# Decoders' attention in a hybrid decoder step: values moving past stationary weights in four column groups, and keys and small weights stored turned

## What is computed

```python
def _stick_breaking_block(q, k, v, q_pos, k_pos, sb_bias):
    z = jnp.einsum('bqhd,bkhd->bhqk', q, k).astype(jnp.float32) * (HEAD_DIM ** -0.5)
    z = z + sb_bias.astype(jnp.float32)[None, :, None, None]
    readable = k_pos[None, :] < q_pos[:, None]
    log_keep = jnp.where(readable, jax.nn.log_sigmoid(-z), 0.0)
    log_after = lax.cumsum(log_keep, axis=3, reverse=True) - log_keep
    weights = jnp.where(readable, jnp.exp(jax.nn.log_sigmoid(z) + log_after), 0.0)
    return jnp.einsum('bhqk,bkhd->bqhd', weights.astype(v.dtype), v)
```

## Time and profile before

| | |
|---|---|
| median of 3 runs | 2342.86 us (2342.21 to 2346.5) |
| profiled execution, whole time | 2343.74 us |
| its span, first to last instruction | 2342.0 us |
| mean granted TensorE clock | 0.88 |
| TensorE, VectorE, ScalarE, GpSimd busy | 79%, 66%, 24%, 55% |
| moved by the DMA | 844.78 MB, mean 361 GB/s |
| chain that ended last | PE 39%, DMA 24%, DVE 15%, POOL 6%, issue 6% |

### The profile page before, as it was taken

One profiled execution on the slowest core, in us unless ns is written; L12 is line 12 of the kernel. 1 busy time (PEld: TensorE's weight loads), 2 busy tenths in 40 slices (PEclk: granted clock), 3 DMA queues, 4 the chain that ended last, 5 costly groups with the idle time before them and its releaser, 6 DMA issues.

```text
span 2342.0 us, 24900 instructions
## 1 busy us (share of the span) xinstructions
PE 1858.9 (79%) x7896; PEld 1299.5 (55%) x7896; DVE 1555.9 (66%) x3451; ACT 557.2 (24%) x1184; POOL 1284.8 (55%) x1197
## 2 busy tenths in 40 slices
PE   4878889788897977979789999777665677677787
PEld 2658878667785755745667577665443222222233
DVE  1211265799878667788787565767789886776652
ACT  1041121566111221246122200110111221122121
POOL 0001044576656566667666435655566677767773
PEclk7999989889998988989987657999787899989999
DMA  8878799999999899999999798999998999999997
GB/s 290 315 278 258 268 334 354 408 357 328 382 411 412 332 402 344 412 411 351 395 410 409 288 312 299 408 394 330 388 404 324 335 386 408 391 409 408 409 409 264
DMA packets 218370, 844.78 MB, mean 361 GB/s; under 512 B 27135, under 2 KB 34615, under 8 KB 196736
## 3 DMA queue, kind: packets, MB, share of 16 engines
q0 software_dynamic: 167168, 605.66, 67.4%
q1 hardware_dynamic: 35044, 215.27, 23.9%
q10 hardware_dynamic: 16028, 22.26, 2.8%
HBM read 826.02 MB, written 16.80 MB: 360 GB/s over the span
## 4 chain that ended last, share of the span: by engine, by line
PE 39%; DMA 24%; DVE 15%; POOL 6%; issue 6%; DVEq 5%; ACT 3%; SPq 1%; ACTq 0%; POOLq 0%
PE bank L855 11%; DMA gather_ring<-in_expert_down,expert_numbers 10%; PE bank L846 9%; PE bank L1224 8%; DMA gather_ring<-in_expert_up,expert_numbers 5%; DVE expert_sums L1994 4%; DMA weight_chunks<-in_w_in 4%; DVE gather_ring L1963 4%; POOL gather_ring L811 3%; POOL gather_ring L796 2%; PE bank L1142 2%; PE bank L1139 1%; DMA v_tokens<-in_expert_up,expert_numbers 1%; DMA weight_chunks<-in_expert_down,expert_numbers 1%; DMA row_tables<-mod_prompt 1%
## 5 line engine op out<-in xcount | busy, mean ns | idle before, releaser
L796 POOL DMA_INDIRECT gather_ring<-in_expert_down,expert_numbers x510 | 588.9, 1155 | 518.3 <-DVE expert_dots L1963 259.8
L1224 PE MATMUL bank<-gather_ring,coef_diagonals 128*128 128x512 f32 x1040 | 575.6, 694 | 270.4 <-DMA gather_ring<-in_expert_up,expert_numbers 164.2
L811 POOL DMA_INDIRECT gather_ring<-in_expert_up,expert_numbers x532 | 570.4, 1072 | 312.1 <-PE bank L1224 145.3
L1963 DVE CUSTOM_DVE_ANT_0 gather_ring<-gather_ring,h_tiles 128x1024 f32<-128x1024 f32 x410 | 500.5, 1226 | 183.5 <-DMA gather_ring<-in_expert_down,expert_numbers 164.3
L1224 PEld LDWEIGHTS bank<-gather_ring,coef_diagonals 128*128 128x128 f32 x1040 | 212.0, 218 | 558.8 <-issue 418.9
L855 PE MATMUL bank<-hT,weight_chunks 128*128 128x128 f32 (+2 forms) x2304 | 401.5, 335 | 29.5 <-DMA weight_chunks<-in_w_in 21.1
L855 PEld LDWEIGHTS bank<-hT,weight_chunks 128*128 128x128 f32 x2304 | 371.7, 197 | 72.3 <-issue 36.5
L1994 DVE SCALAR_TENSOR_TENSOR expert_sums<-gather_ring,expert_coefs,expert_sums 128x1024 f32<-128x1024 f32 x269 | 345.5, 1284 | 8.6 <-issue 8.6
L846 PE MATMUL bank<-weight_chunks,hT 128*128 128x256 f32 x960 | 223.9, 393 | 25.2 <-DMA weight_chunks<-in_w_in 17.3
L846 PEld LDWEIGHTS bank<-weight_chunks,hT 128*128 128x128 f32 x960 | 188.2, 198 | 62.9 <-DMA weight_chunks<-in_w_in 20.3
L1541 ACT ACTIVATE coef_diagonals<-identity,expert_coefs 128x128 f32<-128x128 f32 x304 | 108.6, 395 | 357.6 <-DVE expert_coefs L1974 166.2
(11 more groups left out here) (268 smaller groups left out, 2154.3 us busy)
## 6 DMA issues: line engine op xcount, KB each, us to landing
weight_chunks<-in_w_in SPq DMA_DIRECT2D x84, 1024.0 KB
weight_chunks<-in_w_ada SPq DMA_DIRECT2D x24, 1024.0 KB
weight_chunks<-in_w_query SPq DMA_DIRECT2D x24, 1024.0 KB
weight_chunks<-in_w_branch_a SPq DMA_DIRECT2D x12, 1024.0 KB
weight_chunks<-in_w_branch_b SPq DMA_DIRECT2D x12, 1024.0 KB
weight_chunks<-in_w_out SPq DMA_DIRECT2D x12, 1024.0 KB
gather_ring<-in_expert_up,expert_numbers POOLq DMA_INDIRECT x532, 10.8
weight_chunks<-in_cache_k SPq DMA_DIRECT2D x16, 512.0 KB
```

The lines of the kernel that those rows point to most:

```text
L796: pool.indirect_dma_start(out=d_row(slot), out_offset=None, in_=down, in_offset=bass.IndirectOffsetOnAxis(ap=expert[:, t, h * TOPK + k:h * ...
L811: pool.indirect_dma_start(out=u_row(slot), out_offset=None, in_=up, in_offset=bass.IndirectOffsetOnAxis(ap=expert[:, t, h * TOPK + k:h * T ...
L1224: mm = nc.tensor.matmul(bank[6 + half], diag[:, n % 8, :], u_row(slot)[:, half * 512:(half + 1) * 512], start=(u == PE_TILE[t][0]), stop=( ...
L1963: nc.vector.tensor_tensor_reduce(out=row, in0=row, in1=x, scale=1.0, scalar=0.0, op0=ALU.mult, op1=ALU.add, accum_out=dots[:, m % 2, k:k + ...
```

## The change

1. The host stores `cache_k`, `w_spatial` and `sub_keys` turned, so that a page of keys arrives with the head's channels on the partitions. `turn_page`, the copies of `page_turned`, `turn_small` and the copies behind them are gone; `page_scores` reads the page in the weight buffer. The corner blocks are 8 loads instead of 16, straight into their place, and VectorE masks both in place.
2. The values' products change their operands: for each decoder, each half of the heads and each of three parts of keys, four products with 32 columns of weights stationary (those of four decoders, of which one is wanted) and 128 columns of values moving write four column groups of 32 partitions, one for each head. ScalarE sets the banks aside (`set_aside`), TensorE turns them, and 16 small copies pick the wanted blocks into `qT`. TensorE waits for them before the mix.
3. The exponents are three pieces instead of one, the costs in `pieces` are new, and two pieces "turn values" follow the values.

```diff
     if g == LASTG:
-        out += [("past scores", 9)] * NDEC + [("own scores", 6), ("exponents", 8)] + [("past values", 7)] * NDEC
+        out += [("past scores", 5)] * NDEC + [("own scores", 6)] + [("exponents", 7)] * 3
+        out += [("past values", 3)] * NDEC + [("turn values", 4)] * 2
...
-        ws_nat = U[:, 0:1024].rearrange("p (g s) -> p g s", g=NH)
-        wss_nat = U[:, 1024:2048].rearrange("p (g s) -> p g s", g=NH)
-        sk_nat = sg[:, 2, 0:256].rearrange("p (a d) -> p a d", a=2)
...
-        turned_page = [kT[:, j].rearrange("p h d -> p (h d)") for j in range(2)]
         kTf = kT[:, 2].rearrange("p h d -> p (h d)")
         pos_s = [kTf[:, 0:512], kTf[:, 512:1024], vv[0:NS, 2, 0:512]]
         neg_s = [vv[:, 0, 0:512], vv[:, 0, 512:1024], vv[0:NS, 2, 512:1024]]
-        log_s = [vv[:, 1, 0:512], vv[:, 1, 512:1024], turned_page[0][0:NS, 0:512]]
+        log_s = [vv[:, 1, 0:512], vv[:, 1, 512:1024], kT[0:NS, 0].rearrange("p h d -> p (h d)")[:, 0:512]]
+        side_s = [kT[:, 2 * n + 1].rearrange("p h d -> p (h d)") for n in range(2)]
...
                 elif phase == "keys":
-                    sp.wait_ge(s_ktf[1], 2 * c + 2)
+                    sp.wait_ge(s_sz, c + 1)
...
-            const(nc.gpsimd.memset(wss_nat, 0.0))
+            const(nc.gpsimd.memset(small_rows[0:NS, :], 0.0))
...
-            def turn_small(c):
-                if c == 0:
-                    pe.wait_ge(s_small, 16 * NSMALL)
-                    pe.wait_ge(s_wss, 16 * (P // DSEQ))
-                for half in range(2):
-                    if c < 2:
-                        turn_four(4 + 2 * c + half, [(ws_nat, wss_nat)[c][:, 4 * half + j, :] for j in range(4)])
-                    elif c == 2:
-                        turn_four(8 + half, [sk_nat[:, half, :]])
...
-                    def turn_page(m_):
-                        n = NUMBER["keys", g, m_ // 2]
+                    for b in range(NDEC):
+                        n = NUMBER["keys", g, b]
                         weight(n)
-                        page = row_of(n, m_ % 2)
-                        for half in range(2):
-                            if m_:
-                                pe.wait_ge(s_kte, 2 * (m_ - 1) + half + 1)
-                            for j in range(4):
-                                mm = nc.tensor.transpose(bank[2 + half][:, j * P:(j + 1) * P],
-                                                         page[:, (4 * half + j) * P:(4 * half + j + 1) * P], ident[:])
-                            mm.then_inc(s_ktf[half], 1)
-                    def page_scores(m_):
-                        b, page = m_ // 2, m_ % 2
-                        pe.wait_ge(s_kte, 2 * m_ + 2)
-                        for hd in range(NH):
-                            at = hd * NS + b * DSEQ
-                            mm = nc.tensor.matmul(bank[4 + page][:, at:at + DSEQ],
-                                                  turned_page[m_ % 2][:, hd * P:(hd + 1) * P],
-                                                  q[:, hd, P + b * DSEQ:P + (b + 1) * DSEQ], start=False,
-                                                  stop=(b == NDEC - 1 and hd == NH - 1))
+                        for page in range(2):
+                            for hd in range(NH):
+                                at = hd * NS + b * DSEQ
+                                mm = nc.tensor.matmul(bank[4 + page][:, at:at + DSEQ], row_of(n, page)[:, hd * P:(hd + 1) * P],
+                                                      q[:, hd, P + b * DSEQ:P + (b + 1) * DSEQ], start=False,
+                                                      stop=(b == NDEC - 1 and hd == NH - 1))
                         mm.then_inc(s_sz, 1)
-                    for b in range(NDEC):
-                        for m_ in (2 * b, 2 * b + 1):
-                            turn_page(m_)
-                            if m_:
-                                page_scores(m_ - 1)
                         yield
-                    page_scores(2 * NDEC - 1)
...
-                    mm.then_inc(s_scm, 1)
-                    yield
+                        mm.then_inc(s_scm, 1)
+                        yield
                     pe.wait_ge(s_sw, 1)
                     for b in range(NDEC):
                         n = NUMBER["values", g, b]
                         weight(n)
-                        for hd in range(NH):
-                            at = slice(hd * NS + b * DSEQ, hd * NS + (b + 1) * DSEQ)
-                            nc.tensor.matmul(bank[4][:, at], vv[0:NS, SAMPLE, hd * P:(hd + 1) * P], log_s[2][:, at],
-                                             start=True, stop=False)
-                            for page in range(2):
-                                mm = nc.tensor.matmul(bank[4][:, at], row_of(n, page)[:, hd * P:(hd + 1) * P],
-                                                      log_s[page][:, at], start=False, stop=(page == 1))
+                        out = bank[2 + b // 2]
+                        for r in range(2):
+                            cols = slice((2 * (b % 2) + r) * P, (2 * (b % 2) + r + 1) * P)
+                            for part in range(3):
+                                for j in range(4):
+                                    hd = 4 * r + j
+                                    mine = slice(hd * NS + 32 * (b // 4), hd * NS + 32 * (b // 4) + 32)
+                                    keys = vv[0:NS, SAMPLE, :] if part == 2 else row_of(n, part)
+                                    mm = nc.tensor.matmul(out[32 * j:32 * j + 32, cols], log_s[part][:, mine],
+                                                          keys[:, hd * P:(hd + 1) * P], start=(part == 0), stop=(part == 2))
                         mm.then_inc(s_sv, 1)
                         yield
+                    for half in range(2):
+                        pe.wait_ge(s_side, half + 1)
+                        for r in range(2):
+                            for b in range(4):
+                                mm = nc.tensor.transpose(bank[2 + 2 * half + r][:, b * P:(b + 1) * P],
+                                                         side_s[half][:, (2 * b + r) * P:(2 * b + r + 1) * P], ident[:])
+                        mm.then_inc(s_st, 1)
+                        yield
+                if SAMPLE in tiles:
+                    pe.wait_ge(s_se, 1)
...
-                            if SAMPLE in tiles:
-                                pe.wait_ge(s_se, 1)
...
+                pe.wait_ge(s_small, 16 * NSMALL)
...
-            act.dma_start(ws_nat, w_spatial.rearrange("l g t s -> t (l g) s")).then_inc(s_small, 16)
+            act.dma_start(WsT[:], w_spatial.rearrange("l s g t -> s (l g) t")).then_inc(s_small, 16)
             act.wait_ge(s_cond, 16 * 2)
             nc.scalar.activation(c9, c9, ACT.Silu).then_inc(s_silu, 1)
-            act.dma_start(sk_nat, sub_keys.rearrange("l a k d -> k (l a) d")).then_inc(s_small, 16)
...
-            act.wait_ge(s_zero, 1)
-            for b in range(P // DSEQ):
-                act.dma_start(wss_nat[b * DSEQ:(b + 1) * DSEQ, :, b * DSEQ:(b + 1) * DSEQ],
-                              w_spatial[0, :, 0:DSEQ, 0:DSEQ].rearrange("g t s -> t g s")).then_inc(s_wss, 16)
+            act.wait_ge(s_const, NCONST)
+            for b in range(NDEC):
+                act.dma_start(WsTs[b * DSEQ:(b + 1) * DSEQ, :, b * DSEQ:(b + 1) * DSEQ],
+                              w_spatial[0, 0:DSEQ, :, 0:DSEQ]).then_inc(s_wss, 16)
...
-                    def page_turned(m_):
-                        if m_ >= 2:
-                            act.wait_ge(s_sz, m_ - 1)
-                        for half in range(2):
-                            act.wait_ge(s_ktf[half], m_ + 1)
-                            nc.scalar.copy(turned_page[m_ % 2][:, half * 512:(half + 1) * 512],
-                                           bank[2 + half][:, :]).then_inc(s_kte, 1)
                     for b in range(NDEC):
-                        for m_ in (2 * b, 2 * b + 1):
-                            page_turned(m_)
                         yield
                     act.wait_ge(s_sn, 1)
                     act.wait_ge(s_vst, 16 * TILES)
@@ -1455,17 +1418,35 @@
                         ins = nc.scalar.activation(log_s[part], log_s[part], ACT.Ln, bias=1.0)
                     ins.then_inc(s_sl, 1)
                     yield
-                    act.wait_ge(s_scm, 1)
+                    yield
+                    yield
+                    act.wait_ge(s_scm, 3)
                     for part in range(3):
                         rows = NS if part == 2 else P
                         ins = nc.scalar.activation(log_s[part], bank[(2, 3, 1)[part]][0:rows, :], ACT.Exp, scale=-1.0)
                     ins.then_inc(s_sw, 1)
                     yield
+                    def set_aside(half):
+                        act.wait_ge(s_sv, 4 * half + 4)
```

(33 more changed lines are left out.)

19 lines of the change are left out of this document (6 added, 13 removed).

## The result

| | before | changed |
|---|---|---|
| median, this comparison | 2344.55 us (4 runs) | 2315.77 us (2303.82 to 2318.92, 4 runs) |
| ratio, 95% interval | | 0.9867 (0.9834 to 0.9900) |
| profiled execution, whole time and span | 2343.74, 2342.0 | 2318.92, 2317.2 |
| ratio in two later comparisons | | 0.9877 (0.9836 to 0.9918), 0.9892 (0.9847 to 0.9938) |

What follows compares the result with a forecast made beforehand. Transfers bound the kernel until 1289 us, then gathers waited for TensorE. Decoders' stages 169 us plus 36 for moved events, 205 against 235, less 2 given back, plus 2 at the beginning: 2343.7 - 30 = 2314 us, range 2292 to 2338.

Steps and rivals of the forecast that it cites:

- the likeliest case: Whole kernel: the forecast of 2314 us, taken as 2300 to 2324 us, with chance 0.5.
- The bound of 47 us: Stages from 1289 us on: time transfers lost against 409 GB/s, 10 + 29 + 8 us, the most a cure returns.
- the 13 events: Decoders' stage squeezed from 52 events (two gathers each) to 39; the other 13 go to stages around it, 36 us.
- The price of 2.8 us an event: Stages around the decoders': cost of each added event, between 2.56 us bound by bytes and 3.4 with everything on it.
- Page scores: Page-score stage without transposes: 0.21 us a record at half clock, 72 us for 14 events, TensorE the bound by 16 us.
- The forecast of a rate under 380: Page-score stage: transfers under 380 GB/s, with a granted clock under 0.65, would show TensorE as the bound.
- Own scores and exponents: Stage between page scores and values, exponents cut in three: 38 us; the 10 us lost there go to about 5.
- Values: Values' stage with swapped operands: 61 ns a record, 3.4 us a batch; the bytes bound it at 41 us.
- Turns and waits: Behind the values: set-aside copies, 16 transposes, small copies and TensorE's wait before the mix, taken as 18 us.
- the loss of 8 us behind them: Mix and what follows: transfers' loss of 8 us against 409 GB/s, kept; 2 us of gain given back there.
- The beginning: Start of the kernel, small weights stored turned: between 0 and 3 us gained, taken as 2.
- The fourth case: Values: column groups do not run side by side, 0.21 us a record, stage 95 us, whole 2368 us; chance 0.06.

Runs made afterwards that it cites:

- the two repeats: The changed kernel itself, unaltered, run again in two later comparisons: 2317.28 us (4 runs) and 2319.97 us (6 runs).
- the kernel with 128 columns: Kernel before, with the values' products moving 128 columns (two heads' weights), same loads, right placing left out: 2313.16 us, ratio 0.9883.
- the padded kernel: Changed kernel, with page scores moving 64 columns, a decoder's eight queries padded with zeros: 2306.81 us, ratio 0.9825; once more 2312.96 us.
- the repeat: Second run of the changed kernel with zero-padded queries (64 moving columns in the page scores): 2312.96 us, ratio 0.9858.

## Why the prediction was right, and where it was not

**The whole** was right: 2314 forecast, 2315.8 measured, 30 us forecast and 28.8 found, inside the likeliest case. The bound of 47 us held: 27 of them came back. But in part it was right by luck: two errors of the sum stand against each other. TensorE's first page score and the mix (the mix after is above, at 1382.07):

```profile
1196.46 1.09 PE L1086 MATMUL bank<-identity,weight_chunks 128*128 128x128 f32 x8
1430.63 3.76 PE L1159 MATMUL bank<-spatialT,u_and_gv 128*128 128x128 f32 x16
...
1218.43 12.67 PE L1067 MATMUL bank<-qT,weight_chunks 128*128 128x8 f32 x64
```

The decoders' stages took 234.2 us before and 163.6 after, where 169 had been forecast (158.8 and 168.3 in the two repeats). Everything outside them took 2107.8 us before (2108.2 in the kernel with 128 columns, which has the same schedule) and 2153.6 after (2154.6 and 2150.6 in the repeats): 43 to 47 us more for the 13 events that went there, 3.3 to 3.6 us each, where 36 in all had been forecast. That is over the 3 us an event that the prediction itself named as a sign of being wrong. The price of 2.8 us an event was too low, and it was covered by stages that came out shorter.

**Page scores:** clock and record were right. 0.213 us a record against 0.21, a clock of 0.51, a stage of 74 us against 72. TensorE was busy in 74 of 74 us, nearly all of it at the lower level. By the rule of the Trainium skill cited in the prediction ("TensorE: Matmul & The Clock Gate", "Why this matters for your kernels") that work should have had the full rate; for products with 8 moving columns the trace disagrees a second time. What failed is the count of events in the stage, and with it the bytes. The gathers of L809 in the same stretch:

```profile
1218.00:1292.00 74.00, 23.68 (x19) 0.51 1.01 394
```

There are 19, not 14. Two of the five are a miscount: the batches stand at events 232 to 246, but the piece behind them at 248, so the stage is 16 events, and TensorE indeed made six sum rows in it, as it does in 16 events. By the other three the gathers ran ahead of TensorE, for which the ring has room; in the earlier trace rows there were 28 gathers too, for the 25 events from 226 to 251. So the stretch moved 394 GB/s and lost 2.7 us, not 16. The forecast of a rate under 380 was wrong. The price of the half clock wasn't nothing, but it lay mostly behind the stage: 9 us of the whole, by the padded kernel.

**Own scores and exponents:** 37.7 us against 38. The loss there, said to go from 10 to 5 us, stayed at 9.6.

**Values:** the size was off, on the safe side. A batch took 1.85 us at full clock and 3.2 at half, against 3.4 taken at full; that is 0.039 a record with all row changes, nearer to the 30 ns of the halved width than to the 61 taken. That the transfers would then bound the stage was right: 39 us against 41, with 11.4 us of waiting for chunks and 7.3 of the gathers for sum rows, under the 15 set; the rate was 376 GB/s and not near 400. But the reason given, products side by side, was one of several that suffice. Without column groups a batch takes 5.7 us and the time is the same within the spread; with the old loads and 128 moving columns it takes 8.4, at full clock, and the time is still the same. What had to go was the time of before, 11.8 us a batch and 3.76 a sum row at half clock. Full clock alone does it at 8.4 us a batch. Short batches do it too, and need no full clock: the changed kernel has 0.74 in this stage, and its three sum rows took 3.68, 1.98 and 3.06 us, 9 together, as the prediction had them.

**Turns and waits:** 12.6 us (1369.5 to 1382.1) against 18, and the loss of 8 us behind them, which the sum had kept, is 4 in the 95 us from 1385. **Pieces spread over other events:** the sum took 36 us for 13 events, and they cost 43 to 47. With the old costs the decoders' stages take 206.3 us (1203.25 to 1409.54 in its profile) and everything else 2109.9: the 13 events cost about the same inside the stages, 43 us, as outside. So the spacing made no difference that the runs tell, and the whole reckoning by 39 and 52 events was a detour to a right sum. The loss of the transfers by stage, done once for before and once for after, would have said it more plainly.

**The beginning:** 2 us forecast, not distinguishable from nothing.

**The fourth case,** groups that don't overlap, was both untrue and mispriced: with one column group a record takes 0.119 us instead of 0.039, and even so the clock is 0.97, a batch 5.7 us, and the median shows no loss. The prediction had priced it at half clock, 10 us a batch.

## To carry to other kernels

Where TensorE's products move few columns, look at the granted clock of the stretch before counting instructions: the same 48 products took 11.8 us with 8 columns moving at half clock and 8.4 with 128 at full, and the sum rows behind them took 3.76 and 1.88 us. Price a stage by what its bound loses, stage by stage, before and after; work taken from an engine in a stage that the transfers fill (128 transposes here) brings nothing. Here it may even have cost: with the transposes gone the clock fell from 0.72 to 0.57, and the kernel with only the pages turned and their costs lowered was 0.4% slower; whether the clock or the schedule did it stays open.

## What the runs showed of the hardware that was not expected

- Where products with 128 stationary and 8 moving columns filled a stretch, with the sum rows between, the granted clock was 0.51 to 0.59 over 66 to 109 us, though TensorE was idle for 1 us at most in them; with 128 moving columns in the same loop it was 1.00 over 80 us, and with 32 stationary and 128 moving in one column group 0.97 over 55 us.
- 64 moving columns lay between: 0.67 in the values, where the rows change between 64 and 128; in the page scores 3.68 us a batch, full clock, for most batches behind the second, but 6.92 for one of them in the repeat. What makes the difference stays open.
- Four column groups of 32 with 128 moving float32 columns take 0.039 us a record at full clock, one group 0.119 at a clock of 0.97, both with the row changes.
